# Four extra products of constants on TensorE ahead of the fourth S5 output's wait

## The reference, cut to what matters

```python
def s5_mixer(u, a_re, a_im, log_step, b_re, b_im, c_re, c_im, d_skip, w_glu):
    ...
    _, states = lax.associative_scan(combine, (a_seq, bu), axis=1)
    y = jnp.einsum('gcp,btgp->btgc', c_mat, states).real + d_skip.astype(f32) * uf
    z = jax.nn.gelu(y.reshape(bsz, t_len, S5_WIDTH)).astype(u.dtype)
    return z * jax.nn.sigmoid(z @ w_glu)
```

## Time and profile before

| what | value |
|---|---|
| time, median of 3 runs | 2596.72 us |
| the three runs | 2595.74, 2596.72, 2600.99 us |
| the profiled execution's own time | 2599.6 us |
| its span | 2597.8 us |
| mean granted TensorE clock | 0.948 |
| PE busy | 2257.4 us, 87% |
| DVE busy | 1211.5 us, 47% |
| bytes read from memory | 659.36 MB, 254 GB/s over the span |

### The profile page before, as it was taken

The page is one execution under the profiler, slowest core; times in us unless marked ns, Lnnn a source line. Parts: engine busy times, 40 slices in busy tenths (PEclk is TensorE's granted clock), DMA queues, the critical chain, the costliest instruction groups (busy, mean ns, idle before and its releaser), DMA issues.

```text
span 2597.8 us, 38789 instructions
## 1 busy us (share of the span) xinstructions
PE 2257.4 (87%) x17182; PEld 1714.3 (66%) x17182; DVE 1211.5 (47%) x1731; ACT 926.3 (36%) x1331; POOL 1.4 (0%) x6
## 2 busy tenths in 40 slices
PE   8998666667989666667999999999999999999998
PEld 7773122222744211222899999989989999988997
DVE  4543212121873111110665688655456547866554
ACT  4141000001232000000555477554354546865543
POOL 0000000000000000000000000000000000000000
PEclk9999888888999888887999999999999999999999
DMA  7419999999268999999644443445444434434442
GB/s 284 163 51 378 427 429 427 428 428 427 117 252 363 428 427 427 428 428 428 233 166 159 182 147 130 167 182 187 178 169 170 168 133 176 151 142 163 178 180 105
DMA packets 48062, 662.99 MB, mean 255 GB/s; under 512 B 5328, under 2 KB 5584, under 8 KB 7824
## 3 DMA queue, kind: packets, MB, share of 16 engines
q1 hardware_dynamic: 47664, 659.17, 63.2%
q0 software_dynamic: 224, 1.26, 0.1%
HBM read 659.36 MB, written 1.05 MB: 254 GB/s over the span
## 4 chain that ended last, share of the span: by engine, by line
PE 59%; DMA 26%; DVE 6%; ACT 6%; issue 1%; SPq 0%; DVEq 0%; ACTq 0%
DMA ring<-w_dram 26%; PE ps L2463 8%; PE ps L2465 8%; PE ps L2464 8%; PE ps L1919 3%; PE ps L878 3%; PE ps L1342 2%; PE ps L2723 2%; PE ps L2724 2%; PE ps L2725 2%; PE ps L910 2%; PE ps L3329 1%; PE ps L3327 1%; PE ps L3328 1%; ACT r L2440 1%
## 5 line engine op out<-in xcount | busy, mean ns | idle before, releaser
L2451 DVE TENSOR_TENSOR r<-ring,r 128x1024 fp32r<-128x1024 f32 (+1 forms) x392 | 505.6, 1301 | 343.4 <-ACT r L2440 342.8
L2463 PE MATMUL ps<-r 128*128 128x256 f32 x2112 | 608.5, 288 | 8.2 <-DVE r L2535 5.5
L2464 PE MATMUL ps<-r 128*128 128x256 f32 x2112 | 599.3, 284 | 0.0
L2465 PE MATMUL ps<-r 128*128 128x256 f32 x2112 | 599.2, 284 | 0.0
L2440 ACT ACTIVATE r<-ring 128x1024 fp32r<-128x1024 f32 (+1 forms) x392 | 430.6, 1116 | 272.2 <-PE ps L2465 135.5
L878 PE MATMUL ps<-ring 128*32 128x512 f32 x1952 | 294.2, 735 | 188.1 <-DMA ring<-w_dram 187.9
L2463 PEld LDWEIGHTS ps<-r 128*128 128x128 f32 x2112 | 406.6, 193 | 14.7 <-issue 7.3
L2464 PEld LDWEIGHTS ps<-r 128*128 128x128 f32 x2112 | 406.9, 193 | 0.2
L2465 PEld LDWEIGHTS ps<-r 128*128 128x128 f32 x2112 | 406.7, 193 | 0.0
L878 PEld LDWEIGHTS ps<-ring 128*32 128x32 f32 x1952 | 61.4, 122 | 407.4 <-DMA ring<-w_dram 202.4
L1124 DVE TENSOR_TENSOR arena<-ps,arena 128x512 f32<-128x512 f32 x16 | 11.1, 692 | 440.7 <-PE ps L878 440.7
(11 more groups left out here) (446 smaller groups left out, 3128.9 us busy)
## 6 DMA issues: line engine op xcount, KB each, us to landing
ring<-w_dram SPq DMA_DIRECT2D x302, 2048.0 KB, 23.1
arena<-w_dram SPq DMA_DIRECT2D x6, 2048.0 KB, 14.0
ring<-w_dram SPq DMA_DIRECT2D x4, 1024.0 KB, 4.9
arena<-w_dram SPq DMA_DIRECT2D x1, 1536.0 KB, 7.8
x<-x_dram SPq DMA_DIRECT2D x2, 512.0 KB, 3.9
ring<-w_dram SPq DMA_DIRECT2D x2, 512.0 KB, 13.6
out_dram<-x SPq DMA_DIRECT2D x4, 256.0 KB, 2.0
cst<-w_dram SPq DMA_DIRECT2D x1, 973.0 KB, 24.4
```

The lines of the kernel that those rows point to most:

```text
L2451: v.tensor_tensor(lo, w, hi.bitcast(F32), SUB).then_inc(*S.up(f"lo {s}", *(["free " + name] if last else [])))
L2463: pe.matmul(out, hi[:, k, :], K.HH[:, k, :], start=k == 0, stop=False)
L2464: pe.matmul(out, hi[:, k, :], K.HL[:, k, :], start=False, stop=False)
L2465: r = pe.matmul(out, lo[:, k, :], K.HH[:, k, :], start=False, stop=k == 7)
```

## The change

`outputs(3)` in `odd_pe` issues four products ahead of its wait for "odd z3". Each multiplies the 128 x 128 identity with 512 columns of constants, into all 512 columns of the bank "odd c3", which the first term of the output then overwrites in its 256 columns. They stand behind the wait of `bank()` for the last reader of that bank. Nothing else is changed, and `outputs(0)` to `outputs(2)` stay as they are.

```diff
     def outputs(q):
         p = bank(K, pe, f"odd c{q}", K.high)
+        if q == 3:
+            for _ in range(4):
+                warm(K, pe, p)
         pe.wait_ge(*K.after(f"odd z{q}"))
         for i, (part, x) in enumerate(((0, b.TA), (1, b.TB), (1, b.Y[q % 2]), (0, b.Z[q % 2]))):
             for m in range(4):
```

## The result

Twenty runs of the changed kernel have a median of 2602.84 us (2599.7 to 2605.15), twenty of the kernel before 2597.77 us (2591.86 to 2600.99). The ratio is **1.0020, with an interval of 1.0014 to 1.0026**: the change makes the kernel 5.1 us slower, over twice any loss that one of my mechanisms gave. That is just inside the 5.2 us that I had called the limit of what can be told from no change, but the interval of twenty runs is 0.12% wide and resolves it, and the time lies above the range's 2599.9. The profiled execution of the changed kernel took 2601.48 us, with a span of 2599.7 us; all lines of the code from the edit on stand 3 further down.

The account below looks back on a forecast made before the run. Engines bound it up to moe1's first gate products, transfers from 835.90 us. Terms: 0 (products) - 0.02 (scores) - 0 (gate) - 0 (transfers) = -0.02 us, applied to median 2596.72: 2596.7 us, range 2594.7 to 2599.9.

Parts of the forecast that it names:

- The output and its cover: Odd stage: four products cost 0 beside VectorE's last four passes; fourth S5 output takes 1.93 us instead of 3.57.
- Worth on the path: 0.02 us, bounded by 0 and 0.17: First scores in the odd stage stay at about 739.15, waiting for VectorE's `roped(1)`; gain 0.02 us.
- The gate: Gate's first half at 746.47 stays at half clock behind its own untouched pause; its 1.39 us stay, value 0.
- The transfers: Weight stream after SP's issue starts 1.64 us earlier, but a 1.2 us hole and full buffers follow; value 0, at most 1.64.
- The slower rival: Clock falls in TensorE's rest before the first scores, slowing them: 0.5 to 2.1 us, 2597.2 to 2598.8; chance 0.14.
- the step on issue time: Odd stage: the 16 more instructions are issued while TensorE would idle, so issue time costs nothing.
- wrong altogether: Sign that would refute the prediction: a difference in moe1 or the hybrid stages, which no step reaches.
- the 94% for no change: Whole kernel: chance 0.94 that the time is the same within 0.2%, 5.2 us; 0.03 left on each side.

Follow-up runs that it names:

- e2: Changed kernel plus 60 products on moe1's never taken path, bringing only the branch's target back near its old place: 2602.34 us, ratio 1.0017 to the kernel before.
- e3: Changed kernel plus 60 products on moe0's never taken path, so moe1's branch, hint and target lie 255 instructions further on than before: 2597.51 us, ratio 1.0000.
- e4: Kernel before with the same four products issued in moe1's fourth group instead of the odd stage: 2602.98 us, ratio 1.0014.
- e1: Kernel before plus four products on moe1's never taken path, moving only the branch's target by 16 instructions: 2596.19 us against 2598.10, ratio 0.9997.
- e10: Changed kernel with the branch hint's place marked one group of experts earlier in both mixtures: 2604.85 us, ratio 1.0021 to the kernel before.
- e9: Changed kernel without TensorE's branch hints: 2602.35 us, ratio 1.0025 to the kernel before.
- e7: Kernel before, without the change, plus 40 products of 32 columns in moe0's waits and 43 products on moe0's never taken path: 2593.04 us, ratio 0.9984.

## Why the prediction was wrong

**The output and its cover: right.** The products fit the pause at the full clock (3.60 us for 3.44), the output took 1.93 us, and the scores were where VectorE's `roped(1)` put them. "Worth on the path: 0.02 us, bounded by 0 and 0.17" holds for the start of the scores, 4.95 or 4.96 us in twelve profiles; for their length it was 0.3 in some executions, which one profile could not show.

**The gate: right in sign, its phase missed.** I had its half clock untouched by the edit, and it was. I had taken the 5.11 us from one profile; over twelve it varies by 0.9 us for reasons that the edit has no part in, more than the 0.3 us that the edit can win before it.

**The transfers: right in their value, with one row misread.** SP's issue moved up by 1.71 us against "odd z3"'s pass, for 1.64, and DMA stood still at 802 to 806 us. The hole at 771 us took the lead back, but it was shorter, some 0.9 us (393 and 66 GB/s in its two microseconds) for my 1.2: 773.49 in the earlier trace rows is the issue of a small load into `cst`, and the first up load had gone out just ahead of it, as the last of the three issues that end at 742.15 + 31.30 = 773.45. As DMA stood still later, the value of 0 didn't hang on it.

**The slower rival: its sign came, its price didn't.** In the changed execution the clock did fall to 0.71 and 0.50 during the scores, as this rival said, but the gate's first half started 12.28 us after the pass of "odd z3", as before. And e2 and e3, with the same pause of 1.75 us, kept short scores (0.49 and 0.70 us), and e4, without the products there, had the long gate, 5.58 us. The clock's moments move from execution to execution; up to moe1's positions the time varies by 0.9 us with the products and by 1.2 without.

**What failed is the step on issue time**: "The 16 more instructions are issued while TensorE would idle, so issue time costs nothing either." Their issue indeed cost nothing. Their place did: they push every later instruction of TensorE 15 further on, and with it moe1's branch from 198 to 213, where TensorE has to wait for a packet of code behind it. That costs a pause of 4.8 us and half a microsecond behind it at the low clock, 5.28 us where the prediction had put issue at 0. The trace of before held the warning, and I passed over it: the same branch in moe0, at 221, is followed by 4.89 us of "issue", while moe1's is followed by 0.35. The chain at moe0's exit of the kernel before:

```profile
645.30 0.43 DVE x L1151
645.74 4.89 issue
650.63 2.07 PE ps L686 x2
```

Two equal branches of which one costs 4.9 us are a question that a prediction must ask. I wrote instead that a difference in moe1 or the hybrid stages would be "wrong altogether", and the 94% for no change and the range's end at 2599.9 rest on that.

**What stays open.** That the branch's place decides, and neither its target's nor the stage of the products, is shown by e1 to e4, and e10 adds that the hint's own place doesn't matter in the changed kernel. That the pause is a wait for code is shown by the packets in all sixteen pauses; which code a packet holds isn't. Why it comes in time at 197, 198 and 11 to 118 and late from 203 to 246 isn't shown, nor that the hint has a part in it: e9 took it away only where it is of no use. The table looks like a unit of 256 into which the branch has just passed between 198 and 203, with the fetch starting on entry, so that a branch further in finds it done; that is a guess. The 2.26 us at 246, with the packet sent early, fit it; the single 2.28 at 221, in e4, doesn't: its packet came early as well, and nothing here says why.

## What to carry to other kernels

An added instruction moves all code behind it. In a long program with branches, look at every branch in the trace before costing an edit at nothing: an "issue" pause of some 5 us behind one was a wait for code here, and it can come or go with a few instructions anywhere ahead of it, and padding on a path that never runs tells such an effect from the edit's own. A cold clock on an instruction whose reader waits for another engine is worth little to repair (here nothing to 0.3 us of the output's 1.64), even where the chain of waits names that instruction.

## What the runs showed that I had not expected

The kernel before had a pause to give. Placing moe0's branch at 118 and moe1's at 11, with 40 small products executed in moe0's waits, saves 0.16% (e7, 0.9973 to 0.9994); one pause of 4.9 us is 0.19%. And the clock's return at 739.12 in the earlier trace rows, exactly at the first scores, was chance: of six executions without the products only the kernel before and e1 show it.
